# Weights as the moving operand in the dense stages of a two-layer encoder trunk, with results turned back by TensorE

## The reference, cut to what matters

```python
# x is (1, 256, 2048); all float32
h = x * (1 + scale) + shift                      # adaLN, from c_act @ ada_w
y = even_mixer(h, ...)                           # h @ w_in (2048 x 8192), attention + HGRN2, then o @ w_out (2048 x 2048)
x = layer_norm(ALPHA * x + (1 + gate) * y)
y = square(relu(h @ w1)) @ w2                    # w1 2048 x 8192, w2 8192 x 2048
x = layer_norm(ALPHA * x + (1 + gate) * y)
# layer 1: the same with an S5 scan, gelu, and a GLU: z = g @ w_glu (2048 x 4096); a, b = split(z); y = a * sigmoid(b)
```

## Time and profile before

| | us |
|---|---|
| median of 3 runs | 2728.31 (2724.04 to 2728.58) |
| span of the profiled execution, first to last instruction | 2722.2 |
| TensorE busy in it | 2495.7 |
| VectorE busy | 1870.0 |
| ScalarE busy | 1206.3 |

### The profile page before, as it was taken

The page is one execution under the profiler, slowest core; times in us unless marked ns, Lnnn a source line. Parts: engine busy times, 40 slices in busy tenths (PEclk is TensorE's granted clock), DMA queues, the critical chain, the costliest instruction groups (busy, mean ns, idle before and its releaser), DMA issues.

```text
span 2722.2 us, 43151 instructions
## 1 busy us (share of the span) xinstructions
PE 2495.7 (92%) x17156; PEld 2051.1 (75%) x17156; DVE 1870.0 (69%) x1946; ACT 1206.3 (44%) x1040; POOL 111.0 (4%) x154
## 2 busy tenths in 40 slices
PE   5779999976798999999999985699999999999998
PEld 2358888833686888888888861488788888888886
DVE  6976666678756777777777769767756666555555
ACT  4643333354535333334434456733543333444444
POOL 1021000001002000000000011000020000000000
PEclk9989999987798999999999986899999999999999
DMA  9997888722463888888878839588667777555552
GB/s 289 401 337 262 283 275 284 247 70 94 149 209 123 280 284 276 283 277 287 280 260 282 285 150 235 218 283 280 207 204 236 238 233 232 185 186 184 185 186 76
DMA packets 245356, 635.12 MB, mean 233 GB/s; under 512 B 33186, under 2 KB 34852, under 8 KB 240900
## 3 DMA queue, kind: packets, MB, share of 16 engines
q1 hardware_dynamic: 232548, 579.27, 63.9%
q0 software_dynamic: 9536, 34.48, 3.9%
q10 hardware_dynamic: 3168, 19.92, 1.8%
HBM read 613.83 MB, written 19.79 MB: 233 GB/s over the span
## 4 chain that ended last, share of the span: by engine, by line
PE 77%; DVE 16%; ACT 4%; issue 2%; DMA 1%; SPq 0%; DVEq 0%; ACTq 0%
PE PS L298 48%; PE PS L302 24%; DVE raw L1592 2%; DVE Pb L2062 2%; DVE acc L2057 1%; ACT Pb L1126 1%; DVE wlo L288 1%; DVE X L1664 1%; DVE raw L1596 1%; DMA araw<-in_ada_w 1%; PE PS L1023 1%; PE PS L1048 1%; DVE WF L1596 1%; ACT H L1126 1%; DVE X L1750 0%
## 5 line engine op out<-in xcount | busy, mean ns | idle before, releaser
L298 PE MATMUL PS<-H,whi 128*128 128x512 f32 x5888 | 1861.7, 397 | 25.5 <-DVE wlo L288 9.6
L288 DVE TENSOR_TENSOR wlo<-raw,whi 128x2048 fp32r<-128x2048 f32 x368 | 844.2, 2294 | 676.3 <-ACT whi L284 675.3
L302 PEld LDWEIGHTS PS<-H,wlo 128*128 128x128 f32 x5888 | 1109.9, 188 | 261.1
L284 ACT ACTIVATE whi<-raw 128x2048 fp32r<-128x2048 f32 x368 | 705.1, 1917 | 1211.8 <-PE PS L298 1204.1
L302 PE MATMUL PS<-H,wlo 128*128 128x256 f32 x5888 | 1159.7, 278 | 0.0
L298 PEld LDWEIGHTS PS<-H,whi 128*128 128x128 f32 x5888 | 901.9, 189 | 35.5 <-issue 17.4
L185 DVE SCALAR_TENSOR_TENSOR acc<-araw,cact,acc 128x1024 f32<-128x1024 f32 x240 | 308.2, 1284 | 1.4 <-DMA araw<-in_ada_w 0.9
L1126 ACT ACTIVATE Pb<-PS 128x1024 f32 (+5 forms) x106 | 106.0, 1007 | 62.1 <-PE PS L749 29.3
L1713 DVE TENSOR_TENSOR H<-Pb,H 128x512 fp32r<-128x512 f32 x128 | 87.7, 685 | 0.0
L1126 ACT ACTIVATE H<-Pb 128x512 fp32r (+2 forms) x131 | 82.3, 629 | 6.2 <-DVEq L1989 6.2
L2162 POOL TENSOR_SCALAR X<-X,small 128x256 f32<-128x256 f32 x64 | 64.8, 1030 | 437.9 <-ACT H L1126 419.2
(11 more groups left out here) (308 smaller groups left out, 1374.1 us busy)
## 6 DMA issues: line engine op xcount, KB each, us to landing
raw<-in_mlp_w SPq DMA_DIRECT2D x256, 1024.0 KB, 6.2
araw<-in_ada_w SPq DMA_DIRECT2D x274, 512.0 KB, 4.7
raw<-in_mix_w_in SPq DMA_DIRECT2D x64, 1024.0 KB, 7.7
raw<-in_s_w_glu SPq DMA_DIRECT2D x32, 1024.0 KB, 7.4
acc<-in_ada_w SPq DMA_DIRECT2D x40, 512.0 KB, 8.5
raw<-in_ada_w POOLq DMA_DIRECT2D x32, 512.0 KB, 4.3
raw<-in_mix_w_out SPq DMA_DIRECT2D x16, 1024.0 KB, 5.1
vmat<-Pb ACTq DMA_DIRECT2D x8, 1024.0 KB, 7.9
```

What stands on the lines that cost most here:

```text
L284: nc.scalar.activation(whi[:, s % 2, :], raw[:, s, :], ACT.Copy).then_inc(S("hi_done"), 1)
L288: nc.vector.tensor_tensor(wlo[:, s % 2, :], raw[:, s, :], whi[:, s % 2, :].bitcast(F), ALU.subtract).then_inc(S("lo_done"), 1)
L298: return nc.tensor.matmul(PS[:, b, :], w, H2[:, :, k, :], start=first, stop=last, skip_group_check=True)
L302: return nc.tensor.matmul(PS[:, b, 0:T], w, H2[:, 0, k, :], start=False, stop=last, skip_group_check=True)
```

## The change

**Operands.** The activations become stationary (128 channels x 128 tokens, a tile in two halves `t`), and the weights move, 512 columns at a time. A slab is 24 matmuls of 512 columns. Results have tokens on the partitions: a block fills two banks and not four.

**Blocks.** ACT copies both banks to a buffer `TOK` (the relu is in this copy), TensorE turns it with eight 128 x 128 transposes (`flip`) into two further banks, and ACT copies these to `Pb` (`late`; for the MLP this copy squares). `add_block` and the relu on DVE are gone. The transposes of a block stand ahead of the last slab of the next block; in the gate half of glu ahead of the third slab. ACT's `late` waits for them and stands ahead of the split of the next block's first slab. Out: DVE adds the turned banks into `X`. Glu: ACT applies the sigmoid in the copy out of PSUM, DVE multiplies by the value, and adds from PSUM after the turn.

**Down.** One pass over all 2048 output channels in all eight banks; a slab is 128 rows of w2, 8 KB each, and needs one activation tile. The evacuation between the halves is gone, and each tile is split once. In the last slab the banks finish in pairs; ACT copies a pair (`down_out`), TensorE turns it, DVE adds it into `X`.

```diff
-    def high(b, w, k, first, last=False):
-        return nc.tensor.matmul(PS[:, b, :], w, H2[:, :, k, :], ...)
-    def low(b, w, k, last):
-        return nc.tensor.matmul(PS[:, b, 0:T], w, H2[:, 0, k, :], ...)
+    TOK = PF[:, 15360:16384].rearrange("p (t m) -> p t m", t=2)
+    def tokens(k, t):
+        return Hhi[:, k, t * P:(t + 1) * P], Hlo[:, k, t * P:(t + 1) * P]
+    def product(ps, x, w, first=False, last=False):
+        return nc.tensor.matmul(ps, x, w, start=first, stop=last, skip_group_check=True)
+    def flip(b, src):
+        for x in range(4):
+            for t in range(2):
+                o = (x % 2) * T + t * P
+                last = nc.tensor.transpose(PS[:, b + x // 2, o:o + P], src[:, t, x * P:(x + 1) * P], ident[:])
+        return last
...
+    def block_products(pe, evacs, slabs, b, h=None, sums=None, freed=None, turn=None, at=3):
...
+            if turn and s == at:
+                turn()
             pe.wait_ge(S("lo_done"), slabs + s)
...
+                k, cols = 4 * s + kt, slice(kt * 512, (kt + 1) * 512)
+                for t in range(2):
+                    xh, xl = tokens(k, t)
+                    ps = PS[:, b + t, :]
+                    product(ps, xh, whi[:, s % 2, cols], first=(k == 0))
+                    product(ps, xh, wlo[:, s % 2, cols])
+                    last = product(ps, xl, whi[:, s % 2, cols], last=(k == KT - 1))
             last.then_inc(S("slab_used"), 1)
...
-            return w[bass.ds((i * 8 + 2 * s) * P, 2 * P), half * 1024:(half + 1) * 1024].rearrange(
-                "(a p) m -> p a m", p=P)
+            return w[bass.ds((i * 4 + (32 * half + s)) * P, P), :]
...
+            def turned_block(s, blk, b):
+                def turn():
+                    pe.wait_ge(S("evac_done"), blk + (s.E + 1 + PRIME_EVAC))
+                    pe.wait_ge(S("flip_out"), blk + (s.O + 1))
+                    flip(b, TOK).then_inc(S("flip_T"), 1)
+                return turn
...
+                if opening is None and closing is None:
+                    for t in range(2):
+                        xh, xl = tokens(sl, t)
+                        for x, w in ((xh, whi), (xh, wlo), (xl, whi)):
+                            for m in range(4):
+                                last = product(PS[:, 2 * m + t, :], x, w[:, sl % 2, at(m)], last=True)
...
+                def back(m):
+                    pe.wait_ge(S("down_out"), 4 * layer + m + 1)
+                    flip(2 * m, DOWN_TOK[m]).then_inc(S("down_T"), 1)
...
+            def evac(s, blk, par, dst=TOK, b=0):
                 act.wait_ge(S("slab_used"), blk * 4 + (s.G + 4 + PRIME_USED))
+                if dst is TOK and (s.F or not isinstance(blk, int) or blk):
+                    act.wait_ge(S("flip_T"), blk + s.F)
+                run(dst, PS[:, b + 2 * par:b + 2 * par + 2, :], s.func, sem="evac_done")
+            def late(s, blk):
+                act.wait_ge(S("flip_T"), blk + (s.F + 1))
...
+                run(Pb[:, bass.ds(blk * 4 + s.tile0, 4), :], bank(4, 2).rearrange("p (k t) -> p k t", k=4), s.last,
+                    sem="flip_out")
...
+                    for x in range(4):
+                        kt = 4 * m + x
+                        stt(X[:, kt], PS[:, 2 * m + x // 2, (x % 2) * T:(x % 2 + 1) * T],
+                            G1[:, 2 * layer + 1, kt:kt + 1], X[:, kt], ALU.mult, ALU.add
+                            ).then_inc(S("down_evac"), 1)
```

More of the change, by code:

```diff
@@ L313, in wide_products @@
                 pe.wait_ge(S("h_ready"), 4 * h + s + 1)
[L314 to L334, removed]
-            for kt in range(4):
[L336 to L341, removed]
+            if freed and s == 1:
+                ada_turn(pe, freed, 7)
+            for kt in range(4):
+                k, cols = 4 * s + kt, slice(kt * 512, (kt + 1) * 512)
[5 more added lines that the diff above has]
+                    last = product(ps, xl, whi[:, s % 2, cols], last=(k == KT - 1))
             last.then_inc(S("slab_used"), 1)
@@ new lines, in run_block, with body @@
+            def run_block(s, h=None, a_=0, b=4, before=None):
+                def body(i, par, first=False, freed=None, turn=None):
+                    block_products(pe, i * 2 + (s.E + par + 1), i * 8 + (s.G + 4 * par + 1 + PRIME_RAW), a_ + 2 * par,
+                                   None if par else h, s.sums if first else None, freed, turn)
+                body(0, 0, True, None, before and turned_block(before, before.bodies - 1, b))
+                body(0, 1, False, s.sums, turned_block(s, 0, b))
+                with pe.Fori(1, s.bodies // 2) as i:
+                    for par in range(2):
+                        body(i, par, turn=turned_block(s, i * 2 + (par - 1), b))
@@ new lines, in run_gated, with turned_value, turn @@
+            def run_gated():
+                value, gate = plan_glu
+                def turned_value(j):
+                    def turn():
+                        pe.wait_ge(S("glu_value"), j + 1)
+                        if j:
+                            pe.wait_ge(S("x_mixed"), 4 * j)
+                        flip(4, TOK).then_inc(S("flip_T"), 1)
+                    return turn
+                for s in plan_glu:
+                    for blk in range(4):
+                        block_products(pe, s.E + blk + 1, s.G + 4 * blk + 1 + PRIME_RAW, 2 * (blk % 2),
+                                       3 if s is value and blk == 0 else None,
+                                       turn=turned_value(blk - 1) if s is gate and blk else None, at=2)
+                turned_value(3)()
@@ L774, in down_slab @@
+            def down_slab(s, n, i, sl, opening=None, closing=None):
                 pe.wait_ge(S("lo_done"), i * 4 + (s.G + sl + 1 + PRIME_RAW))
                 pe.wait_ge(S("hx_lo"), i * 4 + (n * 32 + sl + 1))
[L776 to L796, removed]
@@ L797, in down_slab, with at @@
-                last.then_inc(S("slab_used"), 1)
-            def run_down(s, n, evacs, freed):
-                for sl in range(4):
[L802 to L810, removed]
+                def at(m):
+                    return slice(512 * m, 512 * m + 512)
@@ new lines, in down_slab @@
+                if opening is None and closing is None:
[4 more added lines that the diff above has]
+                                last = product(PS[:, 2 * m + t, :], x, w[:, sl % 2, at(m)], last=True)
+                    last.then_inc(S("slab_used"), 1)
+                    return
+                for b in (0, 1, 2, 3, 6, 4, 5, 7) if opening else range(8):
+                    m = b // 2
+                    if opening:
+                        opening(b)
+                    xh, xl = tokens(sl, b % 2)
+                    product(PS[:, b, :], xh, whi[:, sl % 2, at(m)], first=opening is not None, last=True)
+                    product(PS[:, b, :], xh, wlo[:, sl % 2, at(m)], last=True)
+                    last = product(PS[:, b, :], xl, whi[:, sl % 2, at(m)], last=True)
+                    if closing and b % 2:
+                        last.then_inc(S("slab_used" if m == 3 else "tile_full"), 1)
+                        closing(m)
@@ L1265, in down_hi, with down_out @@
-                body(0, prev)
+                            ada_copy(act, prev[0].ada[0], 7)
+                        elif opening and sl == 1:
+                            late(*prev)
+                body(0, s.half == 0)
                 with act.Fori(1, 8) as i:
                     body(i)
+            def down_out(layer):
+                s = plan_mlp[layer][1][1]
+                for m in range(4):
+                    if m < 3:
+                        act.wait_ge(S("tile_full"), 3 * layer + m + 1)
+                    else:
+                        act.wait_ge(S("slab_used"), s.G + 32 + PRIME_USED)
+                    run(DOWN_TOK[m], PS[:, 2 * m:2 * m + 2, :], sem="down_out")
```

311 lines of the change are left out of this document (145 added, 166 removed).

## The result

The changed kernel takes 2735.61 us (2732.54 to 2747.41, 8 runs), the kernel before, run beside it, 2726.43 us (2718.77 to 2728.58, 8 runs). The ratio is 1.0041, 95% interval [1.0027, 1.0054]. The forecast was +58 us, 2786 us; some +9 came. The sign was as forecast, the size was not.

What follows compares the result with a forecast made beforehand. TensorE's matmul pace was taken to bound the kernel. Products +6, transposes +53, waits 0, down's halves -7, tails +7, less 1 for glu waits, gave +58 us, 2786 us; the range given was 2658 to 2800 us.

Steps and rivals of the forecast that it cites:

- Products: Dense stages: 24 matmuls of 512 columns a slab at 0.233 us, 5.59 us a slab, +6 us over 368 slabs.
- three readings: Price of 512 contiguous float32r columns: surcharge by columns (+6 us), by runs (-90 us) or none (-147 us).
- the surcharge goes by columns: Matmuls in a slab keep 0.233 us per 512 columns, +6 us; 2786 us for the kernel, chance 0.55.
- one number explains high and low: Reason given for the matmul price: 0.45 ns a column in both the 512- and 256-column forms.
- Case D: Matmul gap near 0.227 us, slab 5.45 us; within a few us of before, 2731 or so; chance 0.07.
- Rival C: Contiguous 512-column reads carry no surcharge, 0.216 us each; -78 us in all, 2650 us; chance 0.16.
- Transposes: Added on TensorE's own list, hidden by nothing: 59 x 8 x 0.112 us, +53 us.
- Their waits: Handoff from a turn to the next block's first slab: slack 0.1 us, cost 0 at 0.233 us a matmul.
- Removed from DVE: 56 adds and 32 relus of about 1.22 us leave VectorE; worth 0.
- Change of halves: Middle of down: TensorE's idle time and the clock drop all go, -7 us.
- Tails: Stage ends: down +3 us a layer, in +1, out +1 at most, glu loses about 1; together +7 us.
- The border: Gap of 512-column matmuls, 0.227 us, under which the forecast said the change wins.

Runs made afterwards that it cites:

- the down-alone kernel: The kernel of before with only the down stages of the change: 2708.94 us, ratio 0.9934; a second time 2708.04 us, 0.9932.

## Why the forecast had the sign and not the size

**Products: the step that failed.** The forecast took the first of three readings, "the surcharge goes by columns", and so 5.59 us a slab and +6 us. Measured: 0.227, 5.44 a slab, 368 x -0.13 = -48 us. That one term is off by 54 us; the whole forecast is off by 49 by the medians, since waits that it put at 0 made up some of it. The reason given for it, "one number explains high and low", did not hold: 512s among themselves cost 0.227, and both prices of before were those of a mixed stream. The 0.45 ns a column is nearly all the columns' own time; the surcharges, 20 ns and 8 ns, stand as 2.5 to 1 and not as 2 to 1. None of the three readings had the cause, since all of them looked for it inside one product, and it lay in its neighbours. Case D, given a chance of 0.07, named the value, without a mechanism. Its sum was written down wrong: -46 + 53 + 4 - 1 is +10, which is 2738 us and not 2731, and that is close to what came.

That the sign was right owes much to luck. The forecast had one large term, +53, and nothing against it. In the runs two terms of that size, -48 and +50, all but cancel, and the sign hung on small ones, the wait that the forecast put at 0 and the tails. Rival C, for which the Trainium skill spoke ("TensorE: Matmul & The Clock Gate", Back-to-back issue gap, 216 ns for 512 columns), does not come about either: even where nothing but 512s follow each other, float32r takes 0.227 here.

**Transposes: right.** Forecast 59 x 8 x 0.112 = +53; measured 0.109 each, and shown by doubling them. By the traces two pair turns a layer start behind the last product, in the tail, and not one, so 57 turns count here: 57 x 8 x 0.109 = +50. The Trainium skill's "TensorE: Matmul & The Clock Gate", PE-mode transpose, gives about 275 ns for a bfloat16 one in a kernel's context. The mean of this group, which is float32, is 274 ns, so it agrees as a latency, but as the price of one more in a row it would be 2.5 times too much.

**Their waits: the chain right, the case not.** wlo stands at F + 6.4 as forecast. Its cost was put at 0 for a slab of 5.59; with a slab of 5.44 the slack is gone, and it takes 0.25 us in most blocks of in and up, by the two wait rows 13 us, of which moving the turn gave back 7 to 8.

**Removed from DVE: 0**, with 153 us of work gone; no run tests it by itself, and the sum below closes without it. **Change of halves: -7, right**: the gap is gone from the chain. **Tails: +7 forecast**; down +2.4 for +3 a layer (looked at in layer 1), in +0.8 for +1, together about +6.

The sum by these: -48 + 50 + 13 - 7 + 6 - 1 = +13 us. The medians differ by 9.2, the profiled executions by 2737.3 - 2722.2 = 15.1. Between two profiled executions some us are not the kernel's: the down-alone kernel had spans of 2711.7 and 2701.8 us with the same dense stretches. In those stretches alone the terms without the tails, +7, stand against +2 measured, so some 5 us of the terms are not placed.

**The border.** The forecast said that the change wins where a gap is under 0.227 us. By its own terms the border is lower: against +53 + 4 - 1 the products must win 0.152 us a slab, which is a gap of 0.226. So 0.227 lies on the losing side, as measured. But one border for the whole hid the lesson: it summed stages of two kinds. A block has 96 products to pay for a turn of 0.87 us and gains 0.50. A down stage has 64 slabs, 1536 products, to pay for four turns, and gains 8 us for 3.5, and the change of halves on top. At the same gap of 0.227, one wins and the other loses.

## What to carry to other kernels

Price a matmul by the starts of a stream of its like: where sizes are mixed, the gaps are those of the mix, and here a form in which all products have 512 columns took 5.44 us for the columns that took 5.57 with 512 and 256 mixed. A transform that adds a fixed piece of work per output tile is decided by how many products share it, so judge and apply it stage by stage; here the down stages alone give 2709 us where the whole change gives 2736. And when a stretch becomes shorter, look again at what it covered: the handoff behind the turn was hidden at 5.59 us a slab and was not at 5.44.

## What the runs showed of the hardware that I had not expected

- float32r products of 512 columns follow each other every 0.227 us at full clock, whether weights or activations move and whether the columns are one run or two; among products of 256 columns they mostly take 0.230 to 0.235, and those of 256 take 0.115 to 0.119, or about 0.12 to 0.13 where one stands alone among 512s while the weights move.
- Four highs and then four lows cost no less than high, low, low, high: 1.40 us for 1.394. The surcharge stays on a 512 that follows a 512, as long as 256s are near.
- The change between transposes and products costs little: from the start of the transposes to that of the next product it is 0.79 us (1108.00 to 1108.79, in the timeline of the changed kernel), and the one after starts 0.32 later instead of 0.227:

```profile
1108.79 0.47 PE L299 MATMUL PS<-whi,H 128*128 128x512 f32 x1
...
1109.11 0.39 PE L299 MATMUL PS<-wlo,H 128*128 128x512 f32 x1
```
